# Second sums of squares gathered while the branch is still being made, and a shifted order of the work at three seams

## The reference, cut to what matters

```python
def rms_norm(x, g):
    xf = x.astype(jnp.float32)
    y = xf * lax.rsqrt(jnp.mean(xf * xf, axis=-1, keepdims=True) + EPS)
    return (y * g.astype(jnp.float32)).astype(x.dtype)

def second_block(...):
    h = x
    h = h + 0.5 * rms_norm(swiglu(rms_norm(h, ffn1_pre_g), ...), ffn1_post_g)
    u = rms_norm(h, mix_pre_g)
    proj = u @ w_in
    ...
    h = h + rms_norm(merged @ w_out, mix_post_g)
    h = h + 0.5 * rms_norm(swiglu(rms_norm(h, ffn2_pre_g), ...), ffn2_post_g)
    ple_gate = jax.nn.sigmoid(rms_norm(h, ple_pre_g) @ w_ple_gate)
    h = h + rms_norm(ple_gate * (p @ w_ple_proj), ple_post_g)
    return h
```

## Time and profile before

| | us |
|---|---|
| median of three runs | 1914.14 |
| lowest and highest run | 1912.59, 1915.74 |
| the profiled execution, its own time | 1913.29 |
| its span, first to last instruction | 1911.1 |
| PE busy in the span | 1839.3 |
| DVE busy | 1097.5 |
| ACT busy | 665.0 |
| PE's mean granted clock, share of full | 0.989 |

### The profile page before, as it was taken

How to read it: one execution, slowest core, us unless ns; L and a number is a source line. 1 busy time by engine, 2 the same in 40 slices (tenths; PEclk the granted TensorE clock), 3 DMA queues, 4 the chain that set the end, 5 groups by cost and what they waited for, 6 DMA issues and landing times.

```text
span 1911.1 us, 23743 instructions
## 1 busy us (share of the span) xinstructions
PE 1839.3 (96%) x8472; PEld 1486.7 (78%) x8472; DVE 1097.5 (57%) x1658; ACT 665.0 (35%) x1010; POOL 175.1 (9%) x125
## 2 busy tenths in 40 slices
PE   6999999999999999999999989999898999999989
PEld 5677888888888888888776767789676888888866
DVE  6565588887334655532353777586666655452265
ACT  4333333323323222222243334565444322222244
POOL 1221000000000000000022334433000000000000
PEclk9999999999999999999999999999999999999999
DMA  4677232333222222233312333231341332233211
GB/s 156 61 82 46 88 112 97 99 99 109 91 97 78 99 99 91 96 112 100 98 67 67 100 113 129 73 110 63 116 144 52 114 99 95 92 121 105 82 64 68
DMA packets 55460, 180.63 MB, mean 95 GB/s; under 512 B 6336, under 2 KB 7104, under 8 KB 55392
## 3 DMA queue, kind: packets, MB, share of 16 engines
q1 hardware_dynamic: 43344, 157.33, 24.8%
q10 hardware_dynamic: 12048, 22.40, 7.4%
HBM read 167.65 MB, written 12.06 MB: 94 GB/s over the span
## 4 chain that ended last, share of the span: by engine, by line
PE 82%; DVE 10%; DMA 3%; ACT 3%; issue 2%; POOL 0%; ACTq 0%; SPq 0%; DVEq 0%
PE bank L790 20%; PE bank L791 20%; PE bank L792 20%; PE bank L812 2%; PE bank L814 2%; PE bank L813 2%; DMA raw<-in_w_proj 2%; PE bank L886 2%; DVE score L2364 2%; PE bank L887 2%; PE bank L888 1%; DVE best L2363 1%; PE bank L861 1%; PE bank L828 1%; PE bank L1221 1%
## 5 line engine op out<-in xcount | busy, mean ns | idle before, releaser
L1309 ACT ACTIVATE w_hi<-raw 128x1024 fp32r<-128x1024 f32 (+2 forms) x281 | 304.4, 1087 | 732.1 <-PE bank L792 627.5
L790 PE MATMUL bank<-a_hi,w_hi 128*128 128x512 f32 x1256 | 494.1, 393 | 11.6 <-DVE w_lo L1922 4.4
L792 PE MATMUL bank<-a_hi,w_lo 128*128 128x512 f32 x1256 | 490.1, 390 | 0.0
L791 PE MATMUL bank<-a_lo,w_hi 128*128 128x512 f32 x1256 | 490.1, 390 | 0.0
L1922 DVE TENSOR_TENSOR w_lo<-raw,w_hi 128x1024 fp32r<-128x1024 f32 (+2 forms) x222 | 284.0, 1279 | 255.7 <-ACT w_hi L1309 242.3
L790 PEld LDWEIGHTS bank<-a_hi,w_hi 128*128 128x128 f32 x1256 | 236.6, 188 | 72.9 <-issue 18.3
L792 PEld LDWEIGHTS bank<-a_hi,w_lo 128*128 128x128 f32 x1256 | 236.6, 188 | 49.6
L791 PEld LDWEIGHTS bank<-a_lo,w_hi 128*128 128x128 f32 x1256 | 236.8, 189 | 48.3
L790 PE MATMUL bank<-h_hi,w_hi 128*128 128x512 f32 x568 | 221.0, 389 | 0.0
L791 PE MATMUL bank<-h_lo,w_hi 128*128 128x512 f32 x568 | 221.0, 389 | 0.0
L792 PE MATMUL bank<-h_hi,w_lo 128*128 128x512 f32 x568 | 220.9, 389 | 0.0
(11 more groups left out here) (312 smaller groups left out, 2171.4 us busy)
## 6 DMA issues: line engine op xcount, KB each, us to landing
raw<-in_w_up SPq DMA_DIRECT2D x132, 512.0 KB, 3.4
raw<-in_w_down SPq DMA_DIRECT2D x48, 704.0 KB, 4.1
raw<-in_w_proj SPq DMA_DIRECT2D x59, 512.0 KB, 3.5
raw<-in_w_wo SPq DMA_DIRECT2D x8, 512.0 KB, 4.2
raw<-in_w_branch SPq DMA_DIRECT2D x16, 256.0 KB, 2.6
gates_in<-spill ACTq DMA_DIRECT2D x16, 256.0 KB, 3.3
raw<-in_w_out SPq DMA_DIRECT2D x8, 512.0 KB, 3.7
raw<-in_w_ple SPq DMA_DIRECT2D x8, 512.0 KB, 3.4
```

The costliest lines, as they stand in the source:

```text
L790: mm(dst[:, :], wh, hi[:, k, :], start=(first and c == 0), stop=False)
L791: mm(dst[:, :], wh, lo[:, k, :], start=False, stop=False)
L792: step = mm(dst[:, :], wl, hi[:, k, :], start=False, stop=(last and c == n - 1))
L1309: fn(w_hi[:, slot, 0:size], raw[:, slot, 0:size], ACT.Copy).then_inc(unit_high, 1)
```

## The change

The sum of squares of the new stream is split by its chunks. For chunks 0 to 5 (`EXPANDED`) it is expanded. With `r` the branch's `rstd` of a token, the sum over channels of (x + r g y)^2 is the sum of x^2, plus 2r times the sum of x g y, plus r^2 times the sum of (g y)^2. The three sums do not need `r`, so they are gathered in the stage in front, in `keep_branch` and `branch_kept`: for each of the six tiles ACT makes one more square (at seam 1 two more, since x^2 is needed there; seams 2 and 3 have it from the seam before, in `stream_sum`), and DVE multiplies `y` by gain and `x` (L2404), adds that to the cross sum (L2410), and adds the new squares. PE contracts these sums in `sum_parts`, behind the branch's `spread` at seams 1 and 2, and at seam 3 in the middle of `pproj`, ahead of `spread("post2")`. Chunks 6 and 7 are squared as before; they are taken first (`SEAM`).

In `add_branch`, DVE adds squares for the first two chunks alone. In the iteration of the fifth chunk (`at == 4`) it puts the parts together in `fold_sums`, five operations on 128x4 numbers, the last of which waits for `total_ready`, the contracted sum of chunks 6 and 7. PE makes that one in `first_three`, after the products of the fourth chunk (`k == 3`), and no longer behind the last. From the fourth chunk on, `a_lo` is made one chunk later: behind the multiplication and the addition of the following chunk.

```diff
+AFTER = {"mixpre": "post1", "pre2": "postmix", "plepre": "post2"}
+SEAM = (6, 7, 0, 1, 2, 3, 4, 5)
+EXPANDED = range(6)
+LAG_FROM = 3
...
+            def sum_parts(split):
+                name, dst = AFTER[split], parts_bank(split)
+                n = tuple(AFTER).index(split)
+                pe.wait_ge(cross_added, DC * n + len(EXPANDED))
+                sum_columns(crosses[name], 0, dst=dst)
+                pe.wait_ge(sum_added, square_at(name + "_branch", EXPANDED[-1]) + 1)
+                step = sum_columns(sums[name + "_branch"], QB, dst=dst)
+                if name == "post1":
+                    pe.wait_ge(sum_added, square_at("post1_stream", EXPANDED[-1]) + 1)
+                    step = sum_columns(sums["post1_stream"], 2 * QB, dst=dst)
+                step.then_inc(parts_ready, 1)
...
+                    if split in AFTER and k == 3:
+                        sum_x(split)
...
-                if not summed:
+                if not summed and split not in AFTER:
                     sum_x(split)
...
             total_x("postmix")
+            wait(tile_read("out", 5))
+            sum_parts("pre2")
             hidden("up3", "pre2", len(AUX))
...
                 if i == 2:
                     sum_x("post2")
+                    wait(tile_read("up3", 0))
+                    sum_parts("plepre")
                 if i == 4:
                     spread("post2")
...
                     square(square_stage, k, tile_bank(stage, k)[:, :], tile_done(stage, k))
                     fn(y[:, k, :], tile_bank(stage, k)[:, :], ACT.Copy).then_inc(tile_sem(stage, k), 1)
+                    if k in EXPANDED:
+                        square(square_stage + "_branch", k, y[:, k, :], tile_read(stage, k), prm(g, k))
+                        if square_stage == "post1":
+                            square("post1_stream", k, x[:, k, :], (x_ready, DC))
...
+            def fold_sums(split):
+
+                parts, r = parts_bank(split), inverse[:, 0:QB]
+                dve.wait_ge(parts_ready, 1 + tuple(AFTER).index(split))
+                step(v.tensor_tensor(folding, parts[:, QB:2 * QB], r, ALU.mult))
+                step(v.scalar_tensor_tensor(folding, parts[:, 0:QB], 2.0, folding, ALU.mult, ALU.add))
+                step(v.tensor_tensor(folding, folding, r, ALU.mult))
+                before = parts[:, 2 * QB:3 * QB] if split == "mixpre" else stream_sum
+                step(v.tensor_tensor(stream_sum, folding, before, ALU.add))
+                dve.wait_ge(total_ready, SUM[split] + 1)
+                v.scalar_tensor_tensor(folded, stream_sum, 0.0, stat_bank[:, 0:QB], ALU.max, ALU.add).then_inc(
+                    folded_ready, 1)
...
-                    if k and split:
-                        add_square(split[0], k - 1)
-                    if k < DC and split:
+                    if at and split and order[at - 1] not in EXPANDED:
+                        add_square(split[0], order[at - 1])
+                    if split and at < LAG_FROM:
                         scaled_low(split[0], split[1], k)
-                    if k in units:
-                        split_unit(units[k])
+                    elif split and at > LAG_FROM:
+                        scaled_low(split[0], split[1], order[at - 1])
+                    if at in units:
+                        split_unit(units[at])
+                    if at == 4 and split:
+                        fold_sums(split[0])
...
                     if k < DC - 1 or square_stage not in LAST_ON_PE:
                         add_square(square_stage, k)
+                    if k in EXPANDED:
+                        wait(tile_read(stage, k))
+                        step(v.scalar_tensor_tensor(chunk[:, k % 2, :], y[:, k, :], prm(g, k), x[:, k, :], ALU.mult,
+                                                    ALU.mult))
...
+                        add_square(square_stage + "_branch", k)
+                        if square_stage == "post1":
+                            add_square("post1_stream", k)
```

More of the change, by code:

```diff
@@ L871, in total_x, with tile_part, part @@
                 spread(name)
-            def first_three(stage, split, hi=a_hi, lo=a_lo):
[L878 to L890, removed]
+            def tile_part(stage, split, i, at, hi=a_hi, lo=a_lo):
+                first, k = UNIT[stage][0], chunks_of(split)[at]
+                if at == 0:
+                    wait_bank(stage, i)
+                    pe.wait_ge(unit_split, first + i + 1)
+                dst, cols = tile_bank(stage, i), slice(k * P, (k + 1) * P)
+                wh, wl = w_hi[:, (first + i) % SLOTS, cols], w_lo[:, (first + i) % SLOTS, cols]
+                mm(dst[:, :], wh, hi[:, k, :], start=(at == 0), stop=False)
+                mm(dst[:, :], wh, lo[:, k, :], start=False, stop=False)
+                step = mm(dst[:, :], wl, hi[:, k, :], start=False, stop=(at == DC - 1))
+                if at == DC - 1:
+                    step.then_inc(unit_done, 1)
+            def first_three(stage, split, hi=a_hi, lo=a_lo):
+                def part(i, at):
+                    tile_part(stage, split, i, at, hi, lo)
                 if split in BY_TILE:
@@ L917, in first_tiles @@
                 first_three(stage, split)
-                if not summed:
+                if not summed and split not in AFTER:
                     sum_x(split)
                 done = DC - FOURTH_FROM if split in FOURTH else 0
-                fill(stage, [(3, done, done + (DC - done) // 2)])
+                half = done + (DC - done) // 2
+                for at in range(done, half):
+                    tile_part(stage, split, 3, at)
                 spread(split)
-                fill(stage, [(3, done + (DC - done) // 2, DC)])
+                for at in range(half, DC):
+                    tile_part(stage, split, 3, at)
             def folded_tiles(stage):
@@ L1345, in take_root, with take_folded_root @@
                     root_ready, 1)
+            def take_folded_root(split):
+                act.wait_ge(folded_ready, 2 + tuple(AFTER).index(split))
+                fn(root[:, 0:QB], folded, ACT.Sqrt, bias=prm("eps"), scale=1.0 / D).then_inc(root_ready, 1)
             def load_root_table():
@@ L1364, in scaled_highs @@
             def scaled_highs(stage, g, before, units):
-                for k in range(DC):
-                    act.wait_ge(x_ready, before + k + 1)
+                for at, k in enumerate(SEAM):
+                    act.wait_ge(x_ready, before + at + 1)
                     scaled_high(g, k)
-                    square(stage, k, x[:, k, :], (x_ready, before + k + 1))
-                    if k == 3:
+                    if k not in EXPANDED:
+                        square(stage, k, x[:, k, :], (x_ready, before + at + 1))
+                    if at == 3:
                         unit_high_part(UNIT[units][0] + 3)
-                take_root(stage, D)
+                    if at == 5:
+                        take_folded_root(stage)
                 for n in range(2):
@@ L1830, in _ @@
                 keep_pproj(i)
-            for k in range(DC):
-                act.wait_ge(x_ready, 3 * DC + k + 1)
+            for at, k in enumerate(SEAM):
+                act.wait_ge(x_ready, 3 * DC + at + 1)
                 scaled_high("ple_pre_g", k)
-                if k < 3:
-                    keep_pproj(5 + k)
-                square("plepre", k, x[:, k, :], (x_ready, 3 * DC + k + 1))
-                if k < 2:
-                    unit_high_part(UNIT["ple"][0] + 2 + k)
-            take_root("plepre", D)
+                if k not in EXPANDED:
+                    square("plepre", k, x[:, k, :], (x_ready, 3 * DC + at + 1))
+                if at < 3:
+                    keep_pproj(5 + at)
+                if at < 2:
+                    unit_high_part(UNIT["ple"][0] + 2 + at)
+                if at == 5:
+                    take_folded_root("plepre")
             for n in range(2):
```

81 lines of the change are left out of this document (54 added, 27 removed).

## The result

The changed kernel takes 1923.88 us, median of ten runs (1918.21 to 1927.31), against 1913.82 for the kernel before in the same comparison: a ratio of 1.0046, 95% interval 1.0037 to 1.0054. It is slower, as forecast, but by nearly 10 us and not by 5, and the time lies above the range of 1915.2 to 1922.0. The profiled execution took 1923.26 us.

A forecast was written before the change was run, and what follows sets the result against it. PE was taken to bound the kernel, busy 96%. Seams -0.1 - 0.1 + 1.5 plus clock falls of 3.2 to 4.8 gave +4.5 to +6.1 us, middle 5.2: 1919.3 us against 1914.14, range 1915.2 to 1922.0.

The forecast's parts named there:

- What bounds the kernel: Whole kernel: PE, busy in 96% of the span; time is saved only where PE waits or its work can go.
- the work in front: Stages ahead of the seams: added DVE work of 2.0 to 2.6 us per expanded tile is covered; taken as nothing.
- The round trip: Seams: DVE's fold waits 1.4 us (over 2 at seam 3) for PE's contraction, then PE idles 2.5 us.
- Case 3: Seams: the fold doesn't wait and the clock holds; -1.4 us at seams 1 and 2, 1910.4 us; chance 0.05.
- The clock behind the fifth chunk's gap: Each seam: products behind PE's new gap run at 1.2 GHz, costing 1.6 us a fall, 3.2 to 4.8 in all.
- Three falls in four: Each seam: chance 3 in 4 that the clock falls behind the new gap, from six of eight earlier waits.
- -0.1 + 1.6: Seams 1 and 2, each: -0.1 us for chunks saved against the round trip, plus 1.6 us for a clock fall.
- nothing, with 0.8 us to spare: Seams 1 and 2: sum_parts' 2.7 and 1.8 us behind the spread fit PE's 3.48 us gap at no cost.
- the sign that I had named: Seams 1 and 2, profile after: the first gap is filled with contractions, its end unmoved.
- +1.5 us: Seam 3: contractions delay the spread and DVE by 1.75 us; with the round trip, +1.5 us before the clock.
- a second gap at seam 3: Seam 3: gaps ahead of the fourth and fifth chunks; the second is worth up to 1.2 us more.
- Case 4: `out` stage: work in front piles up and delays a w_lo; up to 3 us more, 1922 to 1925; chance 0.07.

The follow-up runs named there:

- front_only: Changed kernel with the three seams put back, no sum_parts, no fold; only the work in front stays: 1914.58 us, ratio 1.0001 to the kernel before.
- early_total: Changed kernel with the contraction of chunks 6 and 7 behind the third chunk's products instead of the fourth's: 1912.14 us, ratio 0.9985 to the kernel before.
- late_fold: Changed kernel with fold_sums at the seventh chunk instead of the fifth and the root later, PE's order untouched: 1911.87 us, ratio 0.9988 to the kernel before.
- front_s12: Kernel before plus the work in front everywhere and sum_parts at seams 1 and 2 alone, no fold: 1915.56 us, ratio 1.0009.
- no_lag: Changed kernel with LAG_FROM = DC, every a_lo directly behind its own chunk's addition: 1918.72 us, ratio 1.0025 to the kernel before.
- front_parts: Kernel before plus the work in front and sum_parts at its three places, seams as before, no fold: 1918.15 us, ratio 1.0019.
- parts_gap: Changed kernel with seam 3's sum_parts behind the second chunk's products, in PE's idle time, with its own sum buffer: 1920.29 us, ratio 1.0029 to the kernel before.
- parts_behind: Changed kernel with seam 3's sum_parts moved from ahead of spread("post2") to right behind it: 1923.83 us, ratio 1.0043 to the kernel before.
- early_behind: Changed kernel with chunks 6 and 7 contracted one chunk sooner and seam 3's sum_parts behind spread("post2"): 1910.98 us, ratio 0.9987 to the kernel before.

## Why the prediction was right and wrong

**What bounds the kernel, the work in front**: right. front_only is the kernel before to 0.1%.

**The round trip**: right in its mechanism and nearly in size. In the first profile L2082 idles 1.51 us at seam 2 and 2.63 at seam 3 (forecast 1.4 and over 2), and PE waits 2.42 us at each seam (2.5). At seam 1 L2082 idles 2.36 us, since PE came to the fourth chunk late from the seam's head; there the clock held behind the gap. So seam 1 met its forecast there partly by luck, with a delay that the sum did not have in place of the clock that it had. What the sum lacked is that slow products ahead of the contraction lengthen the fold's wait, as the 4.22 us of the second profile show. Case 3, the fold without a wait, was priced at 1910.4, and early_total and late_fold measured 1912. The forecast had said that the order of PE leaves no way round the wait; there was one, on DVE.

**The clock behind the fifth chunk's gap**: right. Of the twelve gaps of 2.42 us in the four profiles with a waiting fold, eleven were followed by products at 0.63 us. Three falls in four looks too few, though eleven of twelve doesn't exclude it; the changed kernel itself has two of three and three of three. The section of the Trainium skill that the prediction cited (TensorE: Matmul & The Clock Gate, Why this matters for your kernels), read strictly, would have left the clock alone here; the traces decide against that reading. Per seam the sum, -0.1 + 1.6, met 1.1 to 1.8 us at seam 1 and fell short at seam 2, 1.9 to 2.5. There DVE waits 1.72 and 2.17 us for the spread, in place of 1.25: a slow spread is 0.5 and 0.9 us of it, and the rest, 1.4 and 1.5 us, is the forecast.

**`sum_parts` at seams 1 and 2, "nothing, with 0.8 us to spare"**: wrong at seam 1, the smaller miss. The 2.7 us were taken at the upper clock. In the changed kernel's first profile the second and the third contraction there run at the lower one, 1.71 us from start to start in place of 0.81, and hold PE until 955.34, 0.88 us past the start that the first chunk would have had: 954.66, less the 0.20 us by which this profile's seam begins sooner. The first gap's end moved, against the sign that I had named. The price depends on what follows: here the fold waits 0.87 us longer than in the second profile, where 0.66 us of delay were absorbed, and front_s12 absorbed 0.83. At seam 2 the first product was never later than the slow spread alone makes it, to 0.04 us.

**Seam 3, "+1.5 us"**: this step failed, and most of the miss is here. The delay of the spread was put at the contractions' plain length, 1.75 us. The spread came 7.02 us behind the start of the first contraction, against 1829.68 - 1826.02 = 3.66 us before: 3.36 us more, and 8.28 us, 4.62 more, in the second profile. The difference is the clock, which falls in `pproj` behind three contractions in a row though PE never idles: in no_lag, the one profile in which it held there, the delay is 1.79 us, the forecast's. The prediction looked for falls of the clock behind idle time only. front_parts shows that price alone, 3.9 us in its profile, and parts_gap takes it away. Seam 3 cost 4.4 and 7.6 us in all, where the sum had 1.5 + 1.6 = 3.1, and 1.2 more at its upper end. Of the 3.2 us between the two profiles, half is the spread, which DVE gets 1.6 us later, and half the fold's wait, 4.22 against 2.63.

**The sum.** Forecast +5.2 (the middle of 4.5 to 6.1 is 5.3); measured 1923.88 - 1914.14 = +9.7. The table gives +7.5 and +11.8, mean 9.6. With the clock's 4.0 us shared out over the seams, of the 4.5 us missed about 3 are seam 3, 1 is seam 2 and hardly any seam 1. The range failed since its upper end knew of a second gap at seam 3 but of no fall without one. Case 4, a pile-up of the work in front, would have given 1922 to 1925, the measured time; front_only shows that it doesn't happen, so the number would have been right for a wrong reason.

**Open**: what decides whether a given gap brings the clock down. The same 3.3 us gap did and didn't, in two profiles of one kernel. Nor is it known why the spread at seam 2 is slow in some profiles, or whether the contractions behind it have a part in that.

## What to carry to other kernels

When a sum is taken off the vector engine by folding it in later, look at where the folding engine waits: an instruction of 0.16 us with a wait for PE in it held up a whole chunk of work and cost 11 to 12 us over three seams, with the clock behind it, and two chunks later it waits for nothing. Price one-column products on TensorE twice, once by their length and once by the clock of what follows, and put them where PE idles anyway. And before a difference in an unchanged stretch is explained, take a second profile of both kernels.

## What the runs showed of the hardware that I had not expected

- Three contractions in a row (x24 in the rows, one column each, 2.6 us, PE busy throughout) were followed by products at 1.2 GHz in five of six profiles that have them in `pproj` (changed twice, front_parts, early_total, late_fold; not no_lag). A spread and two contractions, 2.6 us too, were not, in two of two (parts_behind, early_behind).
- At the lower clock a contraction takes 1.71 us to the next start, against 0.81 to 0.89: it about doubles, while a product of 512 columns goes from 0.23 to 0.43.
- A spread at the lower clock reads 2.07 us in place of 1.16, and DVE waits 2.17 us for it in place of 1.25.
- DVE, when it has nothing else to do, idles 0.79 us between its addition to `x` and the `a_lo` that needs ACT's `a_hi` of it. In the kernel before, the addition of a square (0.61 us) covered all but 0.19 of that.
